# A first norm that no longer waits for the modulations, and reciprocals of the root kept in a PSUM bank

## What is computed

```
ml = silu(c) @ w_ada[l] + b_ada[l]          # 9 pieces of 1024: shift, scale, gate of three sublayers
mc = silu(c_ctx) @ w_ada[l] + b_ada[l]      # the same for the context stream
def modulate(x, g, shift, scale):
    return x * rsqrt(mean(x * x) + 1e-6) * g * (1 + scale) + shift

lat = x + position_embedding;  cx = ctx
for l in (0, 1):
    lat += 0.5 * ml[2] * swiglu(modulate(lat, g1, ml[0], ml[1]))      # cx the same with mc
    ...token mixer with ml[3..5], second swiglu with ml[6..8]...
```

## Time and profile before

| | |
|---|---|
| Median of 3 runs | 2736.22 us |
| The profiled execution, its own time | 2737.96 us |
| Its span, first to last instruction | 2736.2 us |
| PE (matmul) busy | 2642.9 us, 97% of the span |
| VectorE, ScalarE, GpSimd busy | 44%, 40%, 32% |
| Mean granted TensorE clock | 0.983 of full |
| First matmul of weight slot 0 | 57.69 us from the span's start |

### The profile page before, as it was taken

How to read it: one execution, slowest core, us unless ns; L and a number is a source line. 1 busy time by engine, 2 the same in 40 slices (tenths; PEclk the granted TensorE clock), 3 DMA queues, 4 the chain that set the end, 5 groups by cost and what they waited for, 6 DMA issues and landing times. The chain is left out here.

```text
span 2736.2 us, 44778 instructions
## 1 busy us (share of the span) xinstructions
PE 2642.9 (97%) x17385; PEld 2347.3 (86%) x17385; DVE 1194.1 (44%) x1807; ACT 1107.9 (40%) x1526; POOL 880.6 (32%) x1092
## 2 busy tenths in 40 slices
PE   6999999999999999999999999888999999999999
PEld 3777778988888777788877789888999999999999
DVE  3222324326753223242222246664445756556744
ACT  2322333534424222234222237535664545446533
POOL 0222321321012223212223215404554445553454
PEclk8999999999999999999999999999999999999999
DMA  6343543330023334323334323413554434542454
GB/s 239 123 172 138 160 149 106 124 139 16 23 87 131 139 138 154 132 100 140 137 135 158 134 103 125 153 56 139 184 189 149 155 138 174 181 181 106 161 183 154
DMA packets 58503, 376.49 MB, mean 138 GB/s; under 512 B 6223, under 2 KB 12007, under 8 KB 14216
## 3 DMA queue, kind: packets, MB, share of 16 engines
q1 hardware_dynamic: 56988, 371.51, 37.7%
q10 hardware_dynamic: 1388, 3.16, 0.7%
HBM read 370.44 MB, written 3.16 MB: 137 GB/s over the span
## 5 line engine op out<-in xcount | busy, mean ns | idle before, releaser
L1797 POOL TENSOR_TENSOR WL<-RAW,WH 128x256 fp32r<-128x256 f32 x1088 | 880.4, 839 | 1843.1 <-ACT WH L1300 1843.1
L1300 ACT ACTIVATE WH<-RAW 128x1024 fp32r<-128x1024 f32 x544 | 545.8, 1051 | 955.5 <-PE PSA L551 936.7
L1820 DVE TENSOR_TENSOR WL<-RAW,WH 128x1024 fp32r<-128x1024 f32 x272 | 337.9, 1242 | 1140.1 <-ACT WH L1300 1139.9
L549 PE MATMUL PSA<-HH,WH 128*128 128x512 f32 (+1 forms) x1664 | 600.5, 361 | 16.8 <-DVE HL L1905 7.9
L550 PE MATMUL PSA<-HL,WH 128*128 128x512 f32 (+1 forms) x1664 | 590.9, 355 | 0.0
L551 PE MATMUL PSA<-HH,WL 128*128 128x512 f32 (+1 forms) x1664 | 590.2, 355 | 0.0
L549 PE MATMUL PSA<-GH,WH 128*128 128x256 f32 (+1 forms) x1664 | 530.0, 319 | 4.8 <-DVE GL L1838 4.8
L550 PE MATMUL PSA<-GL,WH 128*128 128x256 f32 (+1 forms) x1664 | 521.3, 313 | 0.0
L551 PE MATMUL PSA<-GH,WL 128*128 128x256 f32 (+1 forms) x1664 | 521.0, 313 | 0.0
L549 PEld LDWEIGHTS PSA<-HH,WH 128*128 128x128 f32 x1664 | 317.9, 191 | 75.8 <-issue 25.7
L551 PEld LDWEIGHTS PSA<-HH,WL 128*128 128x128 f32 x1664 | 317.8, 191 | 43.7
(11 more groups left out here) (310 smaller groups left out, 3066.3 us busy)
## 6 DMA issues: line engine op xcount, KB each, us to landing
RAW<-in_weights SPq DMA_DIRECT2D x272, 1024.0 KB, 4.8
ADA<-in_w_ada SPq DMA_DIRECT2D x65, 1024.0 KB, 4.8
Zada<-in_w_ada SPq DMA_DIRECT2D x7, 1024.0 KB, 13.3
scratch_bias<-BREL ACTq DMA_DIRECT2D x1, 2048.0 KB
SUMS<-in_c_sums SPq DMA_DIRECT2D x1, 1664.0 KB, 8.5
TB<-scratch_bias SPq DMA_DIRECT2D x1, 1536.0 KB, 10.8
X<-in_x SPq DMA_DIRECT2D x1, 1024.0 KB, 8.6
X<-in_ctx SPq DMA_DIRECT2D x1, 1024.0 KB, 12.4
```

Of the source, the lines that this page charges most:

```text
L549: pe.matmul(out, a_hi, b_hi, start=start, stop=False)
L1300: act.activation(WH[:, j, 4 * h:4 * h + 4, :], RAW[:, j, 4 * h:4 * h + 4, :], ACT.Copy)\
L1797: ins = pool.tensor_tensor(WL[:, j, kb, :], RAW[:, j, kb, :], WH[:, j, kb, :].bitcast(F32), ALU.subtract)
L1820: dve.tensor_tensor(WL[:, j, 0:4, :], RAW[:, j, 0:4, :], WH[:, j, 0:4, :].bitcast(F32), ALU.subtract)\
```

## The change

- SP loads `x` and `ctx` ahead of all modulation groups. The groups come in the order 0, 4, 1, 5, 2, 6, 3, 7, so that each pair gives shift and scale of two feature blocks, a quarter of the norm. Weight slot 0 comes after the fifth group, weight slot 1 last.
- ScalarE does a one-column Sqrt ahead of the squares. Its split of weight slot 0 comes after `HH` of block 0, that of slot 1 after block 7.
- TensorE does the column sums with group 0's rows inside them, then rows and columns up to the rows of position 5 and the columns of position 3. The rest stands inside weight slot 0, ahead of k blocks 1 to 4 (`inside_first_slot`); the first pair of slots is written out ahead of the loop for it.
- VectorE makes the modulations in four quarters (`modulations_of`) and starts the scaling after the first. Rows, quarters and its splits stand between the steps of the norm.
- Norms by stream write the reciprocal to PSUM bank 6 and scale from there.

```diff
@@ -441,6 +441,7 @@
             return 2 if ph["kind"] == "in_odd" and i == 3 else 0
+        FIRST_GROUPS = (0, 4, 1, 5, 2, 6, 3, 7)
         CHAIN = [(0, 2, 3, False), (1, 3, 2, False), (0, 3, 0, True), (1, 2, 1, True), (0, 0, 1, True), (1, 1, 0, True)]
         PIECES = [(d, tb) for d, tb, _, _ in CHAIN] + [(1, 0), (0, 1)]
@@ -455,17 +456,16 @@
                              .rearrange("p (k c) -> p k c", k=KB)).then_inc(w_landed[j], 16)
             def first_ada(i):
-                sp.dma_start(Zada[:, i], T["w_ada"][i].rearrange("p (k c) -> p k c", k=KB)).then_inc(zada_landed[i], 16)
-            first_ada(0)
+                sp.dma_start(Zada[:, i], T["w_ada"][FIRST_GROUPS[i]].rearrange("p (k c) -> p k c", k=KB)).then_inc(zada_landed[i], 16)
             sp.dma_start(POS[:], T["c_pos"]).then_inc(x_landed, 16)
             sp.dma_start(X[:, :, 0:NL], T["x"].rearrange("(k p) t -> p k t", p=P)).then_inc(x_landed, 16)
-            first_ada(1)
             sp.dma_start(X[:, :, NL:2 * NL], T["ctx"].rearrange("(k p) t -> p k t", p=P)).then_inc(x_landed, 16)
-            for i in range(2, 7):
+            for i in range(7):
                 first_ada(i)
-                if i > 4:
-                    weight_load(i - 5, i - 5)
-            sp.dma_start(ADA[:], T["w_ada"][7].rearrange("p (k c) -> p k c", k=KB)).then_inc(ada_landed, 16)
+                if i == 4:
+                    weight_load(0, 0)
+            sp.dma_start(ADA[:], T["w_ada"][FIRST_GROUPS[7]].rearrange("p (k c) -> p k c", k=KB)).then_inc(ada_landed, 16)
+            weight_load(1, 1)
             def setup_loads():
@@ -616,18 +616,13 @@
             def norm(ph):
                 N = ph["tokens"]
-                early = 0 if ph["first"] else KB if ph["by_stream"] else 6
+                early = KB if ph["by_stream"] or ph["first"] else 6
                 if ph["first"]:
-                    first_rows(0)
+                    first_norm(N)
                 for kb in range(early, KB):
                     column_sums(bank(4)[:, 0:N], kb == 0, kb == KB - 1, N)
                 if ph.get("mods"):
-                    if ph["first"]:
-                        for g in range(1, 8):
-                            first_rows(g)
-                            first_columns(g - 1)
-                        first_columns(7)
-                    n.skip(mods_read)
+                    n.skip(mods_read, 4 if ph["first"] else 1)
             def unit_sums(ph, u):
@@ -706,11 +701,15 @@
                     if kb % g_step == 0:
                         pe.wait_ge(gl_ready, gbase + kb // g_step + 1)
-                def body(it, begins=False):
+                def body(it, begins=False, first=False):
                     for j in range(2):
                         slot = it * 2 + (ph["slot"] + j)
                         pe.wait_ge(bank_read[j], it * 2 + (ph["unit"] + BANK_CREDIT))
                         each = h_block if normed and j == 0 else None
+                        if ph["slot"] == 0 and j == 0 and first:
+                            def each(kb):
+                                inside_first_slot(kb)
+                                h_block(kb)
                         if kind == "in_odd":
                             def each(kb, i=2 * it + j):
                                 if i % 2 == 0:
@@ -877,6 +876,9 @@
                 elif ph["ends_by_stream"]:
                     body(0)
                     units_by_stream(ph)
+                elif ph["slot"] == 0:
+                    body(0, first=True)
+                    repeat(pe, ph["slots"] // 2, body, loop, first=1)
                 else:
                     repeat(pe, ph["slots"] // 2, body, loop and not ph["squares"] and not ph["feeds"] and not behind_mixer(ph))
                 if kind == "ffn_up":
@@ -1256,7 +1258,33 @@
             def first_columns(g):
                 pe.wait_ge(rows_copied, g + 1)
-                ada_columns(4 * g, g % 2)
+                if g % 2 == 0 and g:
+                    pe.wait_ge(mods_read, g // 2)
+                ada_columns(4 * FIRST_GROUPS[g], g % 2)
+
+            def first_norm(N):
+
+                for kb in range(KB):
+                    column_sums(bank(4)[:, 0:N], kb == 0, kb == KB - 1, N)
+                    if kb == 3:
+                        first_rows(0)
+                first_rows(1)
+                for g in range(2, 6):
+                    first_columns(g - 2)
+                    first_rows(g)
+
+            def inside_first_slot(kb):
+
+                if kb == 1:
+                    first_columns(4)
+                    first_columns(5)
+                elif kb == 2:
+                    first_rows(6)
+                elif kb == 3:
+                    first_rows(7)
+                    first_columns(6)
+                elif kb == 4:
+                    first_columns(7)
             n.skip(gl_ready, GL_CREDIT)
             sel = PR[:, PRM["sel"]:PRM["sel"] + 2]
@@ -1355,20 +1383,20 @@
                 if ph["by_stream"]:
                     return norm_by_stream(ph)
                 if ph["first"]:
+                    act.activation(RSTD[:, 0:1], PR[:, PRM["sel"]:PRM["sel"] + 1], ACT.Sqrt)
                     n.take(x_ready)
                     for kb in range(KB):
                         square(N, X[:, kb, 0:N])
                 n.take(var_ready)
                 act.activation(RSTD[:, 0:N], RSTD[:, 0:N], ACT.Sqrt).then_inc(std_ready, 1)
-                if ph["first"]:
-                    split_hi(16, 0)
-                    split_hi(16, 1)
                 for kb in range(KB):
                     n.take(t_ready)
                     for s, t in streams(N):
                         ins = act.activation(HH[:, kb, t], T2[:, kb % 2, t], ACT.Identity,
                                              bias=MODS[:, ph["mods"][0], kb, s:s + 1])
                     ins.then_inc(hh_ready, 1)
+                    if ph["first"] and kb in (0, KB - 1):
+                        split_hi(16, kb % 2)
             def ffn_up(ph):
                 N = ph["tokens"]
@@ -1875,17 +1903,36 @@
                     return norm_by_stream(ph, modulations)
                 if mods and not ph["first"]:
                     modulations()
-                n.take(sq_used, KB)
-                inverse_rms(bank(4)[:, 0:N], RSTD[:, 0:N], D, var_ready, std_ready)
+                def rows(g):
+                    dve.wait_ge(ada_used, g + 1)
+                    if g >= 2:
+                        dve.wait_ge(ada_done, g - 1)
+                    dve.tensor_copy(ROWS[:, g % 2, :], bank(5 + g % 2)[:, 0:256]).then_inc(rows_copied, 1)
+
+                def modulations_of(p):
+                    k = slice(2 * p, 2 * p + 2)
+                    dve.wait_ge(ada_done, 2 * p + 2)
+                    v, b = modulation(l, mods[0])
+                    dve.tensor_tensor(MODS[:, mods[0], k], v[:, k], b[:, k], ALU.add)
+                    v, b = modulation(l, mods[1])
+                    dve.tensor_tensor(MT[:, k], v[:, k], b[:, k], ALU.add).then_inc(mods_read, 1)
+                    n.take(mods_read)
+                    g = PRM[ph["gain"]] + KB * l + 2 * p
+                    link(dve.scalar_tensor_tensor(MODS[:, mods[1], k], MT[:, k], 1.0, cols(PR[:, g:g + 2], 2), ALU.add, ALU.mult))
+
                 if ph["first"]:
-                    for g in range(8):
-                        dve.wait_ge(ada_used, g + 1)
-                        if g >= 2:
-                            dve.wait_ge(ada_done, g - 1)
-                        dve.tensor_copy(ROWS[:, g % 2, :], bank(5 + g % 2)[:, 0:256]).then_inc(rows_copied, 1)
-                        if g in (3, 7):
-                            split_lo(g // 4, g // 4)
-                    modulations()
+                    rows(0)
+                    n.take(sq_used, KB)
+                    dve.tensor_scalar(RSTD[:, 0:N], bank(4)[:, 0:N], 1.0 / D, EPS, ALU.mult, ALU.add).then_inc(var_ready, 1)
+                    rows(1)
+                    rows(2)
+                    modulations_of(0)
+                    n.take(std_ready)
+                    link(dve.reciprocal(RSTD[:, 0:N], RSTD[:, 0:N]))
+                    rows(3)
+                else:
+                    n.take(sq_used, KB)
+                    inverse_rms(bank(4)[:, 0:N], RSTD[:, 0:N], D, var_ready, std_ready)
                 hbase = n.at(h_ready)
                 dve.wait_ge(gl_ready, n.at(gl_ready))
                 if hbase:
@@ -1907,12 +1954,24 @@
                     ins.then_inc(h_ready, 1)
                 scaled(0)
+                if ph["first"]:
+                    rows(4)
+                    modulations_of(1)
                 for kb in range(KB):
+                    if ph["first"] and kb in (3, 5):
+                        modulations_of((kb + 1) // 2)
                     if kb + 1 < KB:
                         scaled(kb + 1)
                     lower(kb)
+                    if ph["first"]:
+                        if kb == 0:
```

(11 more changed lines are left out.)

## The result

The changed kernel takes 2718.07 us (median of 4 runs, 2717.44 to 2720.49), against 2735.91 for the kernel before in the same comparison: 17.8 us less, a ratio of 0.9936 (95% interval 0.9919 to 0.9954). I had forecast 2725 and a range from 2719 to 2732; the direction and most of the mechanism were right, the size was too small by 6 to 7 us, and the median lies 0.9 us under the range.

The account below looks back on a forecast made before the run. The prediction took TensorE, busy 97% of the span, as the bound. Gains of 9.8 us at the start and 1.5 in the norms by stream, 11.3 together, gave 2725 us from a median of 2736.22, range 2719 to 2732.

Parts of the forecast that it names:

- The bound: Whole kernel: TensorE, busy 97% of the span, sets the end; other engines are busy under half.
- Part 1: Loads: X ahead of two modulation groups lands at 12.2 us instead of 17.16; the early Sqrt costs nothing.
- Rival (b): X's 1 KB rows, not the queue, pace its load: 1.7 us earlier instead of 5.0; 2728 us, chance 0.08.
- Part 2: First norm up to first main matmul: slot 0 starts at 40.3 us instead of 57.69, 17.4 earlier.
- Part 3: Work moved into slot 0: it takes 21.2 us instead of 13.6, ending at 61.5; 9.8 us of gain left.
- Rival (a): Clock stays low in slot 0, ending at 65 to 69 us; gain 4 to 6, 2730 to 2732, chance 0.16.
- (d): Slower: low clock lasts beyond slot 0; 2742 us if all of slot 1 runs at half clock; chance 0.05.
- Part 4: Norms by stream: scalings from PSUM avoid the long form beside GpSimd, 0.36 us per norm, 1.5 for four.
- rival (c): Shorter waits spare two low-clock spells like the second stream norm's, up to 3.3 us each: gain 17, 2719, chance 0.09.
- Rival (e): PSUM reads make the 64 stream-norm scalings dearer: 2726.5 to 2728 us, up to 2732; chance 0.05.
- The sum: Whole kernel: 9.8 us from the start plus 1.5 from the norms by stream, 11.3 us gained.

Follow-up runs that it names:

- e4: The changed kernel with rows of positions 6 and 7 and columns of 4 and 5 moved ahead of slot 0: 2716.31 us, ratio 0.9938.
- e7: The changed kernel with columns of 4 and rows of 6 ahead of slot 0 and rows of 7 one k block earlier: 2717.06 us.

## Why the prediction was wrong

**The bound (right).** PE is 97% busy in both, and what was won at the start of slot 0 and lost inside it arrives at the end.

**Part 1 (right, a little short).** X was paced by the queue. Squares start at 14.17, forecast 14.7; with X first alone the first main matmul moves by exactly 5.0. Rival (b) is out. The early Sqrt brought its own table load (at 6.54 us, 1.28 long) and no second one before the squares.

**Part 2 (mis-sized by 2 to 3 us).** Slot 0 starts at 37.42 (38.47 in the second profile), not 40.3. The step that failed is the sum of the start chain, in two places. The reciprocal started at 28.87 (29.92), forecast 30.4: the squares began at 14.17 (14.68) and not at 14.7, and the sums with group 0's rows inside them took 10.4 us (10.9), where I had added the rows in full and had 11.1; before, without the rows, it was 10.1. From the reciprocal's start on I had 9.9 us to the first matmul (the 9.5 less 0.5 for the first modulations, plus 0.9 of surcharges); it took 8.55 in both profiles. Of that 1.35, about 0.5 is overlap: VectorE's instructions start before the one ahead has ended by its duration, copies 0.34 and pairs of scalings 0.80 apart, where the groups gave 0.42 and 0.88. Another 0.5 I had added for the rest beside GpSimd, and it fell on nothing, as VectorE's rest of weight slot 0 started first and took 1.22. (The next scaling pair and rest pair took 1.82 each, twice their usual length, but TensorE did not have to wait for them.) The last 0.3 are hand-overs, for which I had 0.4.

**Part 3 (right).** I forecast 21.2 us for slot 0 and the stall at rows of 6 that costs them; it took 21.0 (37.42 to 58.45) and 21.2 in the second profile, with the stall at 3.8 us against "five". Counted from slot 0's start, VectorE copied the rows of 6 after 8.9 us (forecast 9.0), and the clock rose after 8.5 (9.2 in the second profile, forecast 9.5). Experiments e4 and e7 show that the stall was worth 2.8 to 3.2 us of the way to slot 0's end. Rival (a), the clock staying low through slot 0, did not happen, nor did (d).

**Part 4 (the waiting right, the clock put at nothing).** The waiting came as forecast: the long scalings are gone, and TensorE gets a norm's sixth block 0.38 us sooner, 1.5 us for all four, 1.6 where the clock is held up. Only its form differs: the 0.85 us wait goes and the one at the sixth block grows from 1.67 to 2.12, where I had said that this one would shrink. But the norms became 3.8 us shorter in the mean of two profiles, and the three pairs of medians with and without the bank are 3.7 to 4.8, 3.8 and 4.4 us apart. What the term put at nothing is the half clock in these norms: 23.9 us before, 17.1 and 20.5 in the changed kernel. I had it in rival (c) alone, at 0.09. Whether it went because of the bank is open, since X first alone, with its reciprocals in SBUF, also has 17.1. Rival (e) is out. So are the 4 us that the estimate from the Trainium skill (VectorE: DVE Perf Modes, section on the TRN2 errata) would have given back; this case does not show that rule: scalings from PSUM take 481 ns median where those from SBUF took 485, and writing the reciprocal to PSUM takes 1761 instead of 1753 ns.

**The sum.** 12.2 + 3.8 = 16.0 us in the profiles, against 9.8 + 1.5 = 11.3: 2.4 us too little at the start, and 2.3 in the norms. The remaining 1.8 of the measured 17.8 is within what the kernel before varies from batch to batch: in the second comparison the difference is 2734.96 - 2719.09 = 15.9. A gain of 16 us lies inside the range given; 17.8 does not, so where the median fell against the range's low end is partly chance. Rival (c), which set the low end, took a clock gain on top of the start as summed; the range had no room for that gain together with a shorter start chain. It was also added up short: 11.3 and two times 3.3 are 17.9, not 17, which would have put the low end at 2718.3. In rival (a) the slip is alike: its ends of 65 to 69 us for slot 0 give gains of 3.8 to 7.8, not 4 to 6.

## What to carry to other kernels

Sum a chain on one engine by the distances between starts, not by durations; over the dozen or so instructions behind the reciprocal the difference was 0.5 us here, and surcharges for collisions and hand-overs that did not come added 0.8. When TensorE waits repeatedly for another engine, look at the clock as well: useless matmuls in these waits took all the half clock out of the norms, 4.4 us there and 2.9 off the median. Where small steps of a side chain are put between blocks of a main one, each copy has to be reached by its producer before its consumer stands there: the order of the producer's list, not the amount of work, made the 3.8 us stall. And before a change is given credit for clock, look for a profile without the change that has the same clock; here there was one.

## What the runs showed of the hardware

- The same program shows low clock at different places from run to run: 94.6 us of half clock in the profile of before, 64.0 and 70.7 us in two profiles of the changed kernel. The tail, with its code untouched, was between 1098.8 and 1109.4 us long in the fourteen profiles, with 16.0 to 40.0 us at half clock. A difference of under 3 us between two medians of five can therefore be this alone, above all across batches.
- The norms' stretches between reciprocals vary with it in steps: in the kernels without filled waits the second took 22.0 us with 6.8 us at half clock (SBUF), 20.3 to 20.5 with 3.4 (bank), and with none 19.2 or 19.3 (bank) and 19.6 (SBUF).
- Waits of about 2 us are enough for a stretch at half clock to go with them: in the changed kernel's second profile TensorE waits 0.18 and 2.12 us in the second norm, and 3.4 us of half clock begin near the end of the second wait; with the waits filled to 0.18 and 0.45 there is none. The first profile has the same two waits and no half clock, so a wait does not bring it every time.
- The mixer, with the same work, took 323.5 to 323.6 us where 6.8 us of it were at half clock, 325.1 with 10.2, and 326.4 to 326.8 with 13.7. What decides where these stretches fall was not tried.
